# HGRN2 scores in 32-row tiles, state-space decays moved to ScalarE, and state-space outputs in alternating column halves

## The chip, the cores and the metric

The kernel runs on 1 core of one Trainium2 chip. The metric is the device time of one execution in microseconds, lower is better. Engines are named as in the profile: PE is TensorE's matmul side and PEld its weight load, DVE is VectorE, ACT is ScalarE, POOL is GpSimd, SP is SyncE, which issues all DMAs.

## The reference, cut to what matters

A sequence of 512 tokens with 1024 channels goes through two blocks. The first (gated linear attention, a short convolution, sliding-window attention, a gated feed-forward) is not touched by the change. The second puts 16 meta tokens in front, projects, runs two mixers side by side, adds their output projection and runs another feed-forward. The two mixers:

```python
# HGRN2, 8 heads, key and value width 128, f in (0, 1) a forget gate
bcum = cumsum(log f)                       # within a chunk
scores = (q * exp(bcum)) @ (k * exp(-bcum)).T
scores = where(causal, scores, 0)          # s <= r
o_intra = scores @ v
o_inter = (q * exp(bcum)) @ state ; state = exp(blast) * state + k_end.T @ v
...
# Mamba-2 (state space), 16 heads of width 64 in 2 groups, state 128
a_cum = cumsum(dt * a)                     # within a chunk, falling
seg   = a_cum[i] - a_cum[j]
l_mat = exp(where(i >= j, seg, -inf))
y_diag = ((c @ b.T) * l_mat) @ (x * dt)
y_off  = (c @ state) * exp(a_cum) ; state = exp(a_cum[-1]) * state + b.T @ (x * dt * exp(a_cum[-1] - a_cum))
y = (y_diag + y_off + d_skip * x) * silu(z)
```

The kernel takes chunks of 128 tokens for both mixers, and the 16 meta tokens as a chunk of their own.

## The kernel before

**Layout.** Activations lie with channels on the 128 partitions and tokens along the free axis: 512 tokens, or 528 with the meta tokens. All large products run in a split form: each operand is cut into a high and a low part of a reduced 32-bit format (`w_hi`, `w_lo`, `u_hi`, `u_lo`), and three products are summed. The order of all work is one list, `STEPS`, made by `schedule()`: products over one 128-column tile of a weight matrix (a *group*, 8 units of 128 x 128, each unit three products in two halves of 264 columns), with *stages* hung behind chosen groups. Every engine walks the same list and does its own part of each entry, so each engine's queue is in the order of `STEPS`, and semaphores tie the queues together. There is no scheduler behind it.

**Weights.** They stream in slabs of 8 units: SP brings a slab into `w_raw`, ACT rounds it to `w_hi`, POOL forms `w_lo`. ACT does this at the start of a group, two slabs ahead of the slab in use.

**Accumulators.** In the second block the groups alternate between two slots in PSUM banks 0 to 3. The stages use banks 4 to 7.

**HGRN2.** For head n the groups are `hf`, `hq`, `hi`, `hg`, and its stages lie behind the next groups: `prep` behind `hg` of the same head, then, behind `hq`, `hi`, `hg` of the next head and `hf` of the one after, the stages `head_a`, `head_b`, `head_c`, `head_d`. For the last head they lie behind `mb 0`, `mb 1`, `mc 0`, `mc 1`.

- `prep` (ACT, DVE) makes `qd2` (queries times decay) and `KC`: for each block of 128 tokens five matrices of keys, of which the first four are the keys scaled to the four 32-token sub-chunks of queries.
- `head_a` on PE makes the scores in bank 4 (for each block four products, each with a whole 128 x 128 tile of `KC` as the loaded operand and 32 columns of `qd2` as the streamed one), and turns (transposes through the identity) the end keys into bank 5 and the values into bank 6. DVE masks the scores into `h_attn`, key on partitions, query along the free axis. ACT copies the turned keys and values to `h_ktok` and `h_vtok` and reports `tok_ok`.
- `head_b` on PE waits for `tok_ok` and `attn_ok`, then makes the state updates in bank 4; DVE folds them into `h_state`.
- `head_c` on PE makes the output in bank 5 from `h_vtok`, `h_attn`, `h_state` and `qz2`.

All of these products are plain fp32: the trace shows two passes, each a weight load and a matmul, for one product, and one pass for a transpose.

**State space.** For t = 0 to 7, two heads each: group `oh t`, `ssm_a`, group `mz t-1` (not for t = 0), `ssm_gate`, `ssm_b`, group `mx t+1`, `ssm_c`, group `oh t+1`.

- `ssm_a` on PE spreads the cumulated decays of the two heads over all partitions (banks 4 and 5, products with 16 rows) and turns x (bank 6). ACT takes exp of them into `m_er`, and the chunk ends into `m_al` and `m_dec` (`row`). DVE then subtracts the per-partition value and clips at zero, block by block, into `m_at` (L1528, 8 instructions, and L1530 for the meta tokens), and forms `m_dte` and `m_dtm` (`diff`). ACT takes exp of all four (`exp`). DVE, meanwhile, multiplies `m_er` by c, and scales x by dt; behind `exp` it makes the second x tile (`xt`, for which PE's `ssm_b` waits) and multiplies `m_at` by the c-b products (`attn`, for which `ssm_c` waits).
- `ssm_b` on PE makes the state updates, DVE folds them into `m_st` (`state`).
- `ssm_c` on PE makes the outputs of the two heads: head 0 of the pair in PSUM partitions 0 to 63, head 1 in 64 to 127, each with a 64-column loaded operand and 128 streamed columns. Before the change all of head 0 comes first, then all of head 1.

**For comparison in the same program.** The first block has two stages with narrow loaded operands: the GLA scores of `head_a` (two products of 64 output rows, in the lower and the upper half, behind one full one), and `swa_c`, where products of 64 output rows alternate between the halves:

```python
for j in js:
    for g in range(SWA_G):
        lo = slice(SWA_HD * g, SWA_HD * (g + 1))
        last = mm(ps[lo, 3, at:at + BLK], s_vtok[:, b - 1 + j, lo], s_PT[:, 2 * g + i, j, :], ...)
```

`mm(out, lhsT, rhs)` is L541 and `turn` is L545 of the kernel before; in the changed one they are L544 and L548. `f` (ACT's activation) is L822 and L832.

## Time and profile before

| | us |
|---|---|
| median of 3 runs | 1980.67 (1979.62 to 1981.73) |
| the profiled execution, its own time | 1978.91 |
| its span in the profile | 1977.1 |
| PE busy | 1860.9 (94%) |
| DVE busy | 933.3 (47%) |
| ACT busy | 720.7 (36%) |
| POOL busy | 698.2 (35%) |
| mean granted TensorE clock, share of full speed | 0.964 |

The profile is of one execution. Its times are from the start of the span, and its own time is 1.81 us over the span and 1.76 us under the median. In its rows, an engine's line gives the start, the length, the instruction (for PE with rows * columns of the loaded operand and the shape streamed) and in brackets the idle time before it with what ended it. A matmul's length holds its way through the array, so where matmuls follow each other the distance between two starts is what one costs, and that is read from the starts of neighbouring rows. The granted clock is 1.00 at 2.4 GHz and 0.50 at 1.2 GHz.

### The profile page before, as it was taken

To read this page: it belongs to the slowest core of one execution; us is meant where nothing else is said; L and a number is where in the kernel's file an instruction comes from. 1 tells how busy PE (TensorE), PEld (TensorE's weight loads), DVE (VectorE), ACT (ScalarE), POOL (GpSimd) and SP (SyncE) were. 2 spreads that over 40 slices of the span, in tenths; PEclk is the share of its full clock that TensorE was granted. 3 is DMA by queue.
4 is the path that set the end of the run, shared out by engine and by line. 5 is a ranking of instruction groups with operands and counts; after the bars stand their busy time and mean duration, and the time that the engine had idled before them with its cause. 6 is when DMAs were issued, how large, how long until landed. Compare 5 with 4: busy or idle time off the path is not lost.

```text
span 1977.1 us, 26889 instructions
## 1 busy us (share of the span) xinstructions
PE 1860.9 (94%) x11004; PEld 1610.6 (81%) x11004; DVE 933.3 (47%) x1424; ACT 720.7 (36%) x1034; POOL 698.2 (35%) x290
## 2 busy tenths in 40 slices
PE   5999999999999999997899998889998999999997
PEld 3777777778778888886899998778987899999885
DVE  3455523334366656113545455455667265665202
ACT  4444434332343333223346454322332243333221
POOL 2333333344344444442222222212322334444442
PEclk9999999999999999998899998879998999999999
DMA  4222222223223333331221211111211223333331
GB/s 157 75 75 75 75 86 76 85 86 95 87 75 96 96 96 93 99 94 55 65 65 54 73 56 55 54 33 54 65 44 54 75 75 90 93 90 93 96 96 64
DMA packets 44185, 154.15 MB, mean 78 GB/s; under 512 B 5776, under 2 KB 6032, under 8 KB 44064
## 3 DMA queue, kind: packets, MB, share of 16 engines
q1 hardware_dynamic: 44064, 152.44, 25.4%
q8 instruction: 87, 1.43, 0.3%
q14 instruction: 34, 0.28, 0.0%
HBM read 150.33 MB, written 2.10 MB: 77 GB/s over the span
## 4 chain that ended last, share of the span: by engine, by line
PE 83%; DVE 11%; ACT 4%; issue 1%; SPq 0%; ACTq 0%; DMA 0%; DVEq 0%
PE ps L541 81%; DVE arena L1165 4%; ACT arena L822 2%; PE ps L545 2%; DVE full L1311 1%; DVE u_lo L1162 1%; ACT L827 1%; DVE arena L1528 1%; DVE arena L1402 1%; DVE v_hi L1180 0%; DVE arena L1172 0%; DVE h_res L1357 0%; ACTq L1145 0%; DVE arena L1162 0%; ACT r_bc L822 0%
## 5 line engine op out<-in xcount | busy, mean ns | idle before, releaser
L515 POOL TENSOR_TENSOR w_lo<-w_raw,w_hi 128x1024 fp32r<-128x1024 f32 x280 | 690.2, 2468 | 1229.4 <-ACT w_hi L822 1229.3
L541 PE MATMUL ps<-u_hi,w_hi 128*128 128x264 f32 (+3 forms) x2376 | 661.9, 332 | 41.7 <-DVE u_lo L1162 29.9
L541 PE MATMUL ps<-u_hi,w_lo 128*128 128x264 f32 (+3 forms) x2376 | 651.2, 328 | 0.0
L541 PE MATMUL ps<-u_lo,w_hi 128*128 128x264 f32 (+3 forms) x2376 | 648.8, 327 | 0.0
L541 PEld LDWEIGHTS ps<-u_hi,w_hi 128*128 128x128 f32 (+1 forms) x2376 | 403.6, 193 | 98.1 <-issue 44.4
L541 PEld LDWEIGHTS ps<-u_lo,w_hi 128*128 128x128 f32 (+1 forms) x2376 | 403.1, 192 | 37.5 <-issue 0.8
L541 PEld LDWEIGHTS ps<-u_hi,w_lo 128*128 128x128 f32 (+1 forms) x2376 | 404.2, 192 | 35.8 <-issue 1.0
L822 ACT ACTIVATE w_hi<-w_raw 128x1024 fp32r<-128x1024 f32 x280 | 297.0, 1061 | 203.1 <-PE ps L541 167.5
L1172 DVE SCALAR_TENSOR_TENSOR ffn<-ps,par,ffn 128x512 f32<-128x512 f32 (+2 forms) x176 | 132.1, 750 | 192.6 <-ACT ffn L822 187.4
L822 ACT ACTIVATE arena<-ps 128x512 f32<-128x512 f32 (+6 forms) x210 | 91.8, 488 | 323.1 <-PE ps L541 168.0
L541 PE MATMUL ps<-arena 128*64 128x128 f32 (+9 forms) x1212 | 161.0, 289 | 27.9 <-DVE arena L1165 14.6
L541 PEld LDWEIGHTS ps<-arena 128*128 128x128 f32 (+4 forms) x1212 | 139.4, 178 | 51.7 <-issue 18.3
L822 ACT ACTIVATE ffn<-ps,par 128x512 f32<-128x512 f32 x88 | 64.5, 733 | 297.2 <-PE ps L541 297.2
L1165 DVE TENSOR_TENSOR arena<-arena 128x128 f32<-128x128 f32 (+9 forms) x213 | 139.5, 697 | 21.7 <-ACT arena L822 19.8
L1162 DVE TENSOR_TENSOR h_res<-ps,h_res 128x512 f32<-128x512 f32 (+1 forms) x32 | 22.2, 693 | 263.7 <-PE ps L541 263.7
L541 PE MATMUL ps<-a_lo,w_hi 128*128 128x512 f32 x352 | 139.0, 395 | 0.0
L541 PE MATMUL ps<-a_hi,w_lo 128*128 128x512 f32 x352 | 139.0, 395 | 0.0
L541 PE MATMUL ps<-a_hi,w_hi 128*128 128x512 f32 x352 | 139.0, 395 | 0.0
L822 ACT ACTIVATE arena<-arena 128x528 f32<-128x528 f32 (+8 forms) x161 | 77.6, 513 | 154.4 <-DVE arena L1162 81.4
L1180 DVE CAST a_hi<-ffn 128x512 fp32r<-128x512 f32 x44 | 106.3, 2417 | 1.5
L541 PEld LDWEIGHTS ps<-a_hi,w_lo 128*128 128x128 f32 x352 | 66.2, 188 | 15.7
L541 PEld LDWEIGHTS ps<-a_lo,w_hi 128*128 128x128 f32 x352 | 66.2, 188 | 15.7
(129 smaller groups left out, 1528.3 us busy)
## 6 DMA issues: line engine op xcount, KB each, us to landing
w_raw<-weights SPq DMA_DIRECT2D x280, 512.0 KB, 3.6
h_res<-xT SPq DMA_DIRECT2D x4, 512.0 KB, 5.2
outT<-h_res SPq DMA_DIRECT2D x8, 256.0 KB, 2.1
cst<-consts SPq DMA_DIRECT2D x1, 992.0 KB, 9.4
par<-params SPq DMA_DIRECT2D x1, 243.5 KB, 6.8
msk<-cmask SPq DMA_DIRECT2D x1, 64.0 KB, 9.4
h_res<-metaT SPq DMA_DIRECT2D x1, 64.0 KB, 8.6
arena<-w_alpha SPq DMA_DIRECT2D x1, 32.0 KB, 9.1
```

Source lines behind the costliest of these rows:

```text
L515: nc.gpsimd.tensor_tensor(w_lo[:, s % SPL, 0:n], w_raw[:, s % RAW, 0:n], w_hi[:, s % SPL, 0:n], ALU.subtract).then_inc(w_lo_ok, 1)
L541: return nc.tensor.matmul(out, lhsT, rhs, start=start, stop=stop)
L545: return nc.tensor.transpose(out, x, ident[0:k, 0:k])
L822: return nc.scalar.activation(out, in_, func, **k)
L827: nc.scalar.preload_act_table_set("natural_log_exp_and_others")
L1162: return V.tensor_tensor(out, a, b, op)
L1165: return V.tensor_tensor(out, a, b, ALU.mult)
L1172: return V.scalar_tensor_tensor(out=out, in0=a, scalar=s, in1=b, op0=ALU.mult, op1=ALU.add)
L1180: link(V.tensor_copy(hi, x))
L1311: return V.scalar_tensor_tensor(out=out, in0=h_res[:, k, cols], scalar=g, in1=r, op0=ALU.mult, op1=ALU.mult)
L1402: link(V.tensor_tensor_scan(bc2, seg16, lf2, 0.0, ALU.mult, ALU.add))
L1528: V.tensor_scalar(m_at[:, i, b, :], ps[:, 4 + i, b * BLK:(b + 1) * BLK], m_cols[:, 0, b, h0 + i:h0 + i + 1], 0.0, ALU.subtract, ALU.min)
```

## The change

Three edits, all in the second block.

1. **HGRN2 scores.** `head_a` now loads 32 columns of `qd2` and streams the keys: for sub-chunk c the output is rows 32c to 32c+31 of bank 4, and only the 32(c+1) key columns that the mask can keep. The scores come out with the query on the partitions, so DVE masks with `below` (the transposed mask, put beside the old one in `msk`, whose DMA goes from 64 KB to 128 KB). `head_b` on PE turns the four score blocks into bank 5 behind its own products, ACT gets a `head_b` stage that copies them to `h_attnT`, and `head_c` waits for that copy and reads `h_attnT`.
2. **State-space decays.** The ten subtract-and-clip instructions leave DVE. ACT forms them with Relu(-x + bias), reading PSUM: the two of the meta tokens ahead of `row`, the eight of 128 x 128 behind `exp`, then exp with scale -1 over `m_atm` and `m_at`, and reports `decay`, for which DVE waits ahead of its last four products of `ssm_a`. Exp of `m_dte` and `m_dtm` now comes first.
3. **State-space outputs.** `ssm_c` goes block by block and alternates the two heads' halves; the two meta products come at the end.

The first block's code is the same in both kernels, but for the slice of `msk`.

```diff
@@ head_a, PE
-                            q0 = META + at + HG_C * c
-                            mm(ps[:, 4, at + HG_C * c:at + HG_C * (c + 1)], KC[:, b, c * BLK:(c + 1) * BLK],
-                               qd2[:, q0:q0 + HG_C])
+                            q0, n_k = META + at + HG_C * c, HG_C * (c + 1)
+                            mm(ps[HG_C * c:n_k, 4, at:at + n_k], qd2[:, q0:q0 + HG_C], KC[:, b, c * BLK:c * BLK + n_k])
@@ head_b, PE
+                if not gla:
+                    for b in range(NBLK):
+                        last = turn(ps[:, 5, b * BLK:(b + 1) * BLK], h_attn[:, b, :])
+                    last.then_inc(sc_turned, 1)
@@ head_c, PE
+                if not gla:
+                    pe.wait_ge(sc_ok, n - GLA_H + 1)
@@ ssm_c, PE
-                for i in range(2):
-                    rows = slice(M2_P * i, M2_P * (i + 1))
-                    for b in range(NBLK):
-                        out = ps[rows, 4, b * P:(b + 1) * P]
-                        mm(out, m_xt[:, 0, b, rows], m_at[:, i, b, :], stop=False)
-                        mm(out, m_st[:, b, rows], m_er[:, i, META + b * BLK:META + (b + 1) * BLK], start=False)
+                side = [slice(M2_P * i, M2_P * (i + 1)) for i in range(2)]
+                for b in range(NBLK):
+                    out = [ps[rows, 4, b * P:(b + 1) * P] for rows in side]
+                    for i, rows in enumerate(side):
+                        mm(out[i], m_xt[:, 0, b, rows], m_at[:, i, b, :], stop=False)
+                    for i, rows in enumerate(side):
+                        mm(out[i], m_st[:, b, rows], m_er[:, i, META + b * BLK:META + (b + 1) * BLK], start=False)
+                for i, rows in enumerate(side):
                     last = mm(ps[rows, 7, 288:304], m_xtm[0:META, 0, rows], m_atm[0:META, i, :])
@@ head_b, ACT
+                    act.wait_ge(sc_turned, n - GLA_H + 1)
+                    f(h_attnT, ps[:, 5, :].rearrange("p (b t) -> p b t", t=BLK), ACT.Copy).then_inc(sc_ok, 1)
@@ ssm_a, ACT
-                    last = f(m_dec[:, i, :], ends, ACT.Exp)
+                    f(m_dec[:, i, :], ends, ACT.Exp)
+                    last = f(m_atm[0:META, i, :], ps[0:META, 7, 16 * i:16 * i + 16], ACT.Relu, scale=-1.0,
+                             bias=m_colm[0:META, 0, 2 * t + i:2 * t + i + 1])
                 last.then_inc(S["row"], 1)
                 act.wait_ge(S["diff"], t + 1)
-                f(m_at, m_at, ACT.Exp)
-                f(m_atm[0:META], m_atm[0:META], ACT.Exp)
                 f(m_dte, m_dte, ACT.Exp)
                 f(m_dtm[0:META, :], m_dtm[0:META, :], ACT.Exp).then_inc(S["exp"], 1)
+                for i in range(2):
+                    h = 2 * t + i
+                    for b in range(NBLK):
+                        last = f(m_at[:, i, b, :], ps[:, 4 + i, b * BLK:(b + 1) * BLK], ACT.Relu, scale=-1.0,
+                                 bias=m_cols[:, 0, b, h:h + 1])
+                link(last)
+                f(m_atm[0:META], m_atm[0:META], ACT.Exp, scale=-1.0)
+                f(m_at, m_at, ACT.Exp, scale=-1.0).then_inc(S["decay"], 1)
@@ ssm_a, DVE
-                    for b in range(NBLK):
-                        V.tensor_scalar(m_at[:, i, b, :], ps[:, 4 + i, b * BLK:(b + 1) * BLK],
-                                        m_cols[:, 0, b, h0 + i:h0 + i + 1], 0.0, ALU.subtract, ALU.min)
-                    V.tensor_scalar(m_atm[rm, i, :], ...)
...
+                dve.wait_ge(S["decay"], t + 1)
```

PE, `head_a` of the first HGRN2 head, as it stands before (`arena` is the working memory, `cst` the identity, shapes are output rows x columns):

```order
L541 MATMUL ps<-arena 128x32 x4
L545 MATMUL ps<-cst,arena 128x128 x2
L541 MATMUL ps<-arena 128x32 x4
L545 MATMUL ps<-cst,arena 128x128 x2
L541 MATMUL ps<-arena 128x32 x4
L545 MATMUL ps<-cst,arena 128x128 x2
L541 MATMUL ps<-arena 128x32 x4
L545 MATMUL ps<-cst,arena 128x128 x2
L541 MATMUL ps<-arena 16x16
```

The same place in the changed kernel, its first two blocks of four:

```order
L544 MATMUL ps<-arena 32x32
L544 MATMUL ps<-arena 32x64
L544 MATMUL ps<-arena 32x96
L544 MATMUL ps<-arena 32x128
L548 MATMUL ps<-cst,arena 128x128 x2
L544 MATMUL ps<-arena 32x32
L544 MATMUL ps<-arena 32x64
L544 MATMUL ps<-arena 32x96
L544 MATMUL ps<-arena 32x128
L548 MATMUL ps<-cst,arena 128x128 x2
```

The four score products of a block went from four outputs of 128 rows to four of 32 rows, each in its own quarter of the output rows, and the two transposes between the blocks stay. PE, `head_b` of the same head in the changed kernel, with the products of the groups on both sides:

```order
L544 MATMUL ps<-u_lo,w_hi 128x264 x2
L544 MATMUL ps<-arena 128x128 x4
L548 MATMUL ps<-cst,arena 128x128 x4
L544 MATMUL ps<-u_hi,w_hi 128x264 x2
L544 MATMUL ps<-u_hi,w_lo 128x264 x2
```

The row of L548 is new: four transposes between the state updates and the next group. ACT, `ssm_a` of t = 0 before:

```order
L822 ACTIVATE arena<-ps 128x512
L822 ACTIVATE arena<-ps 128x4 x2
L822 ACTIVATE arena<-ps 128x512
L822 ACTIVATE arena<-ps 128x4 x2
L822 ACTIVATE arena<-arena 128x1024
L822 ACTIVATE arena<-arena 16x32
L822 ACTIVATE arena<-arena 128x8
L822 ACTIVATE arena<-arena 16x2
L822 ACTIVATE w_hi<-w_raw 128x1024
```

And in the changed kernel:

```order
L832 ACTIVATE arena<-ps 128x4 x2
L832 ACTIVATE arena<-ps,arena 16x16
L832 ACTIVATE arena<-arena 128x8
L832 ACTIVATE arena<-arena 16x2
L832 ACTIVATE arena<-ps,arena 128x128 x8
L832 ACTIVATE arena<-arena 16x32
L832 ACTIVATE arena<-arena 128x1024
L832 ACTIVATE w_hi<-w_raw 128x1024
```

The small exps of 8 and 2 columns moved ahead of the large one, and eight Relus of 128 x 128 came between; the weight slab's rounding stays behind all of it. PE, `ssm_c` of t = 0 before, ahead of group `oh 1`:

```order
L541 MATMUL ps<-arena 128x128 x4
L541 MATMUL ps<-arena 64x128 x8
L541 MATMUL ps<-arena 64x16
L541 MATMUL ps<-arena 64x128 x8
L541 MATMUL ps<-arena 64x16
```

And in the changed kernel:

```order
L544 MATMUL ps<-arena 128x128 x4
L544 MATMUL ps<-arena 64x128 x16
L544 MATMUL ps<-arena 64x16 x2
L544 MATMUL ps<-v_hi,w_hi 128x258 x2
L544 MATMUL ps<-v_hi,w_lo 128x258 x2
```

The same 16 products now stand in one run, in which the halves alternate, and the two narrow ones stand together behind them.

## Rows read from the trace of the kernel before

**Rows 1.** The page: busy share of each engine, and the chain that ended last.
```profile
PE 1860.9 (94%) x11004; PEld 1610.6 (81%) x11004; DVE 933.3 (47%) x1424; ACT 720.7 (36%) x1034; POOL 698.2 (35%) x290
...
PE 83%; DVE 11%; ACT 4%; issue 1%; SPq 0%; ACTq 0%; DMA 0%; DVEq 0%
```
**Rows 2.** PE's waits from 1290 to 1480 us: us in total, times, longest.
```profile
PE ps L541 <- DVE arena L1172: 7.8, 1, 7.8
PE ps L541 <- DVE arena L1165: 5.1, 5, 1.4
```
**Rows 3.** Timeline of PE, `head_a` of one HGRN2 head.
```profile
1085.15 1.08 PE L541 MATMUL ps<-arena 128*128 128x32 f32 x8 [1.15 <-DVE arena L1165]
1086.07 0.41 PE L545 MATMUL ps<-cst,arena 128*128 128x128 f32 x2
1086.32 0.98 PE L541 MATMUL ps<-arena 128*128 128x32 f32 x8
1087.13 0.41 PE L545 MATMUL ps<-cst,arena 128*128 128x128 f32 x2
...
1089.26 0.42 PE L545 MATMUL ps<-cst,arena 128*128 128x128 f32 x2
1089.61 0.21 PE L541 MATMUL ps<-arena 128*16 128x16 f32 x2
```
**Rows 4.** Timeline of PE, GLA scores: four 64-column passes, then the transposes.
```profile
127.38 0.34 PE L541 MATMUL ps<-arena 128*64 128x64 f32 x4
...
127.65 0.44 PE L545 MATMUL ps<-cst,arena 128*128 128x128 f32 x2
```
**Rows 5.** Timeline of PE: 12 passes inside `ssm_c`, and 14 passes of `swa_c`.
```profile
1336.78 1.47 PE L541 MATMUL ps<-arena 128*64 128x128 f32 x12
...
405.29 0.99 PE L541 MATMUL ps<-arena 128*64 128x128 f32 x14
```
**Rows 6.** Stretches: us, PE busy (instructions), granted clock, DMA share, GB/s.
```profile
1336.51:1340.72 4.21, 4.21 (x38) 1.00 0.28 58
1225.49:1234.32 8.83, 8.80 (x44) 0.50 0.18 61
```
**Rows 7.** Timeline of ACT: the copies ahead of `tok_ok`, then group `hi`.
```profile
1092.79 0.42 ACT L822 ACTIVATE arena<-ps 16x128 f32<-16x128 f32 x2 [1.52 <-DVE arena L1446]
...
1096.03 0.61 ACT L822 ACTIVATE arena<-ps 128x528 f32<-128x528 f32 x1 [1.62 <-PE ps L541]
```
**Rows 8.** Timeline of PE, `ssm_b` and `ssm_c` at t = 2.
```profile
1357.11 1.35 PE L541 MATMUL ps<-arena 16*128 16x128 f32 x8 [1.40 <-DVE arena L1165]
...
1365.74 4.28 PE L541 MATMUL ps<-arena 128*64 128x128 f32 x36
```
**Rows 9.** Timeline of DVE (first three) and ACT (last two) at t = 2.
```profile
1351.35 1.13 DVE L1528 TENSOR_SCALAR arena<-ps,arena 128x128 f32<-128x128 f32 x4 [3.86 <-ACT arena L822]
...
1356.98 3.35 DVE L1165 TENSOR_TENSOR arena<-arena 128x512 f32<-128x512 f32 x4
...
1362.43 1.49 DVE L1172 SCALAR_TENSOR_TENSOR arena<-arena,ps 128x64 f32<-128x64 f32 x6
...
1349.86 1.35 ACT L822 ACTIVATE arena<-ps 128x512 f32<-128x512 f32 x6 [8.18 <-PE ps L545]
1354.02 1.37 ACT L822 ACTIVATE arena<-arena 128x1024 f32<-128x1024 f32 x4 [2.81 <-DVE arena L1162]
```
**Rows 10.** ACT, group with its shape: a 128 x 128 copy out of PSUM.
```profile
L822 ACT ACTIVATE arena<-ps 128x128 f32<-128x128 f32 x1 | 0.3, 277 | 0.1
```
**Rows 11.** Stretches: us, busy of PE, PEld, DVE, ACT, POOL, granted clock, DMA share, GB/s.
```profile
1358.41:1361.82 3.41, 3.41 (x18) 3.41 (x17) 3.14 (x6) 0.00 (x0) 0.61 (x1) 0.50 0.43 151
...
1378.89:1382.30 3.41, 3.41 (x18) 3.41 (x17) 1.68 (x8) 1.35 (x6) 0.00 (x0) 0.50 0.00 0
```
**Rows 12.** The page's DMA issues, KB and us to landing, and ACT at the start.
```profile
msk<-cmask SPq DMA_DIRECT2D x1, 64.0 KB, 9.4
...
15.55 1.06 ACT L822 ACTIVATE w_hi<-w_raw 128x1024 fp32r<-128x1024 f32 x1 [3.60 <-DMA w_raw<-weights]
```

21 lines of the change are left out of this document (12 added, 9 removed).

## The prediction

> **What bounds the kernel now.** I read the page's busy shares and its chain first: TensorE is busy 94% of the span, and 83% of the chain that ended last lies on it [rows 1]. So a change pays where it shortens TensorE's own queue or a wait of TensorE, and nowhere else. Next, PE's waits in the state-space stage [rows 2]: one of 7.8 us, which is `ssm_c` at t = 0 waiting for the state, and five on VectorE's products (L1165), 5.1 us together and 1.4 at most, all ahead of `ssm_b` (the one of t = 2 in [rows 8]). In HGRN2 a wait stands ahead of each `head_a` (1.15 in [rows 3]). Last, the distances between starts inside the stages that are edited.
>
> **Part 1, scores, on TensorE.** From one pair of transposes to the next is 1.06 us (1086.07 to 1087.13 [rows 3]): 0.25 for two transposes, 0.81 for eight passes with 128 loaded columns. After the change a block's eight passes load 32 columns each and write four separate quarters of the output rows. The trace has no 32-row tile; the nearest rows are 64-row tiles in the GLA scores: four passes, 64 columns streamed, two in each half, take 0.27 us from their start to the first transpose (127.38 to 127.65 [rows 4]), as long as two passes of one half, so the halves run beside each other. The widest quarter streams 128 columns in each of two passes. A column costs 0.85 ns: the twelve passes of 128 columns in [rows 5] span 1.47 us, less the 0.27 that one lasts, over 11 steps, is 0.109 us each. So the eight passes of a block cost 0.27 + 2 x 64 x 0.85 ns = 0.38 us if the four quarters run beside each other. A narrow tile behind a full one starts late: two transposes take 0.35 us ahead of one (1089.26 to 1089.61), 0.25 ahead of a full one, so 0.10 more [rows 3]. A block is then 0.38 + 0.25 + 0.10 = 0.73 us against 1.06: 0.33 saved, and over 4 blocks and 8 heads **10.5 us**. Bounds: if the quarters followed each other, the other three would add 2 x (32+64+96) x 0.85 ns = 0.33 us, and nothing is saved; if only neighbours run together, 64 columns twice more is 0.11, and 7 us are saved. I take the full overlap, since both narrow stages of the trace overlap fully, and keep 0 and 10.5 as ends.
>
> **Part 1, what it adds.** Four transposes in `head_b`, at a pass of 0.11 us each: 0.45 per head, **3.6 us** on TensorE, not covered. ScalarE's copy of 512 columns comes behind them, and `head_c` follows a whole group (6 us) later, which hides it. Queued behind it on ScalarE, where it waits for the turned scores some 1.0 us, is the next slab's rounding. That slab is used two groups later, so TensorE does not see it; uncovered it would be 1.6 us per head. A shorter `head_a` brings TensorE to `head_b` earlier, and `head_b` needs `tok_ok`: ScalarE's last copy ends at 1093.21 [rows 7]. TensorE stood at the end of `hi` at about 1095.9; 4 x 0.33 = 1.3 us earlier is 1094.6. No new wait. VectorE's chain to `ready` starts behind `head_c` and `hg`, so the 0.9 to 1.15 us ahead of `head_a` stay.
>
> **The last head** runs `head_a` at the granted clock 0.50: 8.83 us [rows 6], behind a longer wait that stays (it hangs on ScalarE's work for `dt`). At half the clock the same edit saves about twice: **1.1 us** more. Ends 0 and 3, if the clock comes back sooner.
>
> **Part 3, outputs.** `ssm_c` takes 4.21 us [rows 6], 32 passes at 0.109 (3.5) and 0.7 for the four narrow ones and the turns to them. `swa_c` is the same kind of product with the halves alternating: 14 passes span 0.99 us, less 0.27 is 0.72 for seven pairs, 0.11 a pair [rows 5]. So 32 passes are 16 pairs, 1.75 us, and the narrow ones, now together, 0.35: 2.1 us, 2.1 saved, over eight stages **16.9 us**. Ends: 3 (no overlap, only the narrow passes gain) and 17.
>
> Here a page speaks against the change. The trace first: the rows of `swa_c` show pairs of 64-column tiles with 128 rows each at 0.11 us a pair [rows 5]. The Trainium skill's page "TensorE: Matmul & The Clock Gate", Part 3, "The mechanism", says a weight load overlaps running matmuls only when its row group differs, and that matmuls start in strict program order. All these tiles have the same rows, so by that rule nothing in parts 1 and 3 would overlap; what this gives is the first rival. The trace disagrees with it in two stages.
>
> **Part 2, decays.** At t = 2 ScalarE starts at 1349.86, VectorE's subtractions at 1351.35, the last products of `attn` end at 1360.33 [rows 9]: 10.5 us. `xt`, for which `ssm_b` waits, ends at about 1357.0, 7.2 us after the start. VectorE loses ten instructions: 8 in 2.2 us (twice 1.13) and two small ones in 0.2, 2.4 us [rows 9]. ScalarE gains two small Relus ahead of `row`, 0.2 us. So `xt` comes 2.0 to 2.2 us sooner, and every wait ahead of `ssm_b` (1.43 at most) goes: **5.1 us**, lower end 4. The decays: `diff` at about 2.0 us, small exps 0.3, eight Relus at no more than the 0.277 us of a 128 x 128 copy from PSUM [rows 10], 2.2, then 1.1 for the large exp (from the 1.37 of four [rows 9]): `decay` at 5.6 us. VectorE is ready for it at 5.2. So `attn` is at about 9.0 us, 1.5 sooner than before. `ssm_c` at t = 2 starts at 1365.74 [rows 8] and would start 1.4 to 3.1 us earlier; the state, which ended at 1363.92 [rows 9], comes 1.5 earlier, 1362.4. That just suffices; I price it at nothing, with 0.5 us per stage (3.5) as the bad end. At t = 0 the 7.8 us wait is the same VectorE chain and shrinks by 1.5: **1.6 us**, since the next convolution cannot start before ScalarE's part of it, 2.0 sooner.
>
> **The clock.** In the state-space stage the clock falls to 0.50 for 3.4 us seven times between 1320 and 1500. Three of these spells follow directly on a wait of 1.4 us ahead of `ssm_b` (1358.41, 1443.74, 1474.46), four on `ssm_a`, whose products fill 16 rows (as 1378.89) [rows 11]. Each costs half its length, 1.7 us. With the waits the three should go, 5.1 us; that others come or go as the stages shift I cannot exclude. I take **3.4**, ends 0 and 10.
>
> **The start.** `msk` is 64 KB larger [rows 12], in the queue ahead of weight slabs that ScalarE waits for (3.60 us). At the slabs' own landing rate (512 KB in 3.6 us as the page's median) 64 KB is at most 0.45; at the roughly 400 GB/s of that stretch 0.15. I take **0.15** lost.
>
> **Sum.** 10.5 - 3.6 + 1.1 + 16.9 + 5.1 + 1.6 + 3.4 - 0.15 = 34.9 us. The profiled execution of 1978.91 would be 1944.0; it lies 1.76 under the median, so the median should be near 1945.8. I say **1946**.
>
> **Rivals.**
> - *Tiles with the same rows do not overlap* (the rule above). The scores save 0, the outputs 2.9 (narrow passes only), the last head 0: -3.6 + 2.9 + 5.1 + 1.6 + 3.4 - 0.15 = 9.2 saved, 1971. For it: nothing in the rows. Chance 0.04.
> - *Halves overlap, quarters do not.* The quarters would need a pass to overtake up to six others, the halves two; only the latter is in the trace. Scores 0, last head 0: 23.3 saved, 1957. Chance 0.2; with neighbours alone overlapping it is 1950, and that I count with the forecast.
> - *The clock.* The spells of the state-space stage stay or multiply, because `ssm_c` at half its length leaves `ssm_a` a larger share: 3.4 turns into -3.4, 1953. Chance 0.08. Or all spells go: 1939, 0.03.
> - *Each change of tile waits for the one before to drain: slower.* The rows show 0.10 us extra from a full tile to a narrow one [rows 3]. If no overlap came and every change of quarter or half cost x, there are 128 changes in the scores and some 128 in the outputs. The other terms leave 9.2 saved, so from x = 0.036 us it is a loss; at x = 0.10 it is 26 - 9 = 16 us slower, 1997. Against it: `swa_c` changes halves at every product and runs at 0.055 a pass. Chance 0.03.
>
> **Chances and range.** Forecast, 1940 to 1951: 0.62. Quarters not overlapping: 0.20. The clock worse: 0.08, better: 0.03. The page's rule: 0.04; slower: 0.03. The range must reach to the second rival: **1938 to 1958**. A difference of 0.2% (4 us) is about what a measurement of this kernel can tell from no change. Faster 0.96, same 0.01, slower 0.03.
>
> **What would show it.** Right: in `head_a` the transposes of neighbouring blocks 0.73 us apart, `head_b` 0.45 us longer, `ssm_c` near 2.1 us, no wait ahead of `ssm_b`, PE busy lower by 25 to 30 us. The quarters fail if that distance is 1.06 again; the halves fail if `ssm_c` still takes 4 us. A wait of `ssm_c` on the products of `m_at` or on the state at t of 1 or more would say that ScalarE's decays are late. The forecast is wrong above all if the quarters follow each other, or if the low clock shows over more of the state-space stage than before.

## The result and the profile after

The changed kernel takes **1932.03 us** (median of 4, 1930.48 to 1934.71) against 1980.59 for the kernel before in the same comparison (1979.62 to 1981.73): ratio 0.9755, 95% interval 0.9742 to 0.9768. It is 48.6 us faster. The forecast was 34.9 us, 1946, with a range down to 1938, so the sign was right and the size was 14 us too small, outside the range. The profiled execution spans 1931.4 us against 1977.1: 45.7 us, not 48.6, since that of the kernel before is 1.7 us under its median and that of the changed one 1.1 us over.

The page of the changed kernel, engines and chain, answers to [rows 1]:

```profile
PE 1818.5 (94%) x11036; PEld 1557.1 (81%) x11036; DVE 917.6 (48%) x1344; ACT 744.2 (39%) x1122; POOL 698.8 (36%) x290
...
PE 84%; DVE 10%; ACT 3%; issue 1%; SPq 0%; ACTq 0%; DMA 0%; DVEq 0%
```

TensorE is still the bound, and its busy time fell by 42.4 us, not by 25 to 30. PE's waits from 1290 to 1480 us, which answer to [rows 2] (us, times, longest):

```profile
PE ps L544 <- POOL arena L528: 4.0, 1, 4.0
PE ps L544 <- DVE v_lo L1186: 3.4, 2, 2.9
```

All five waits ahead of `ssm_b` are gone (both lines here belong to the end of the stage). `head_a` of a middle head, the timeline of PE (start, us, operation, [idle before]), answers to [rows 3]:

```profile
1077.55 0.43 PE L544 MATMUL ps<-arena 128*32 128x32 f32 x8 [0.86 <-DVE arena L1189]
1077.91 0.44 PE L548 MATMUL ps<-cst,arena 128*128 128x128 f32 x2
1078.27 0.42 PE L544 MATMUL ps<-arena 128*32 128x32 f32 x8
```

A block is 0.72 us long (1077.55 to 1078.27); 0.73 was forecast, 1.06 it was. Now the stretches, each from the start of one stage to the start of the same stage of the next head or pair (us, PE busy, granted clock, DMA share, GB/s). First of the kernel before: first HGRN2 head, second, last head up to `ssm_c` at t = 0, and state-space stages at t = 1 and 2:

```profile
977.37:1016.99 39.62, 38.75 (x267) 0.84 0.13 43
1016.99:1050.93 33.94, 33.08 (x266) 1.00 0.21 63
1225.49:1306.19 80.70, 64.04 (x424) 0.80 0.15 46
1336.51:1365.74 29.23, 27.83 (x202) 0.94 0.18 55
1365.74:1393.56 27.82, 27.82 (x202) 0.94 0.20 58
```

The same of the changed kernel, and last its `ssm_c`, which answers to the first of [rows 6]:

```profile
977.68:1011.91 34.23, 33.36 (x271) 0.95 0.16 49
1011.91:1044.73 32.82, 31.96 (x271) 1.00 0.22 65
1213.44:1288.83 75.39, 58.93 (x428) 0.84 0.16 50
1314.71:1338.87 24.16, 24.16 (x202) 1.00 0.22 66
1338.87:1364.54 25.67, 25.67 (x202) 0.93 0.21 64
...
1338.87:1340.99 2.12, 2.12 (x38) 1.00 0.04 8
```

How to read them: the clock is 1.00 or 0.50, so a stretch of length L with mean c had 2 x (1 - c) x L us of low clock: the first head 12.7 us before and 3.4 after. Over the whole span the clock's own records in the trace add up to 141 us before and 106 after (mean clocks 0.964 and 0.972). Most of what the forecast missed lies in that difference. Where did the 45.7 us between the two spans go?

| stretch | before | after | gained |
|---|---|---|---|
| up to the first HGRN2 head | 977.37 | 977.68 | -0.3 |
| first head | 39.62 | 34.23 | 5.4 |
| six further heads | 208.5 | 201.5 | 7.0 |
| last head, to `ssm_c` at t = 0 | 80.7 | 75.4 | 5.3 |
| from there to `ssm_c` at t = 7 | 202.9 | 175.1 | 27.7 |
| from there to the end | 468.1 | 467.5 | 0.6 |

### The profile page after: what moved, and what is told of

Its sections match the earlier page's. It is cut to its first block, busy times and chain, and to the rows that moved or that the text cites. A ratio compares the mean times of both kernels' runs of the same rounds, so it can differ in the third digit from the quotient of the medians.

```text
span 1931.4 us, 26981 instructions
## 1 busy us (share of the span) xinstructions
PE 1818.5 (94%) x11036; PEld 1557.1 (81%) x11036; DVE 917.6 (48%) x1344; ACT 744.2 (39%) x1122; POOL 698.8 (36%) x290
## 4 chain that ended last, share of the span: by engine, by line
PE 84%; DVE 10%; ACT 3%; issue 1%; SPq 0%; ACTq 0%; DMA 0%; DVEq 0%
PE ps L544 82%; DVE arena L1189 3%; ACT arena L832 2%; PE ps L548 2%; DVE full L1335 1%; DVE u_lo L1186 1%; ACT L837 1%; DVE arena L1426 1%; DVE v_hi L1204 0%; DVE arena L1196 0%; DVE h_res L1381 0%; ACTq L1169 0%; ACT r_bc L832 0%; DMA w_raw<-weights 0%; DVE v_lo L1186 0%
## 5 line engine op out<-in xcount | busy, mean ns | idle before, releaser
L544 PE MATMUL ps<-u_hi,w_hi 128*128 128x264 f32 (+3 forms) x2376 | 656.5, 330 | 42.4 <-DVE u_lo L1186 30.5
L544 PEld LDWEIGHTS ps<-u_hi,w_hi 128*128 128x128 f32 (+1 forms) x2376 | 399.4, 191 | 99.1 <-issue 45.0
L544 PEld LDWEIGHTS ps<-u_lo,w_hi 128*128 128x128 f32 (+1 forms) x2376 | 398.8, 190 | 37.2 <-issue 0.6
L544 PEld LDWEIGHTS ps<-u_hi,w_lo 128*128 128x128 f32 (+1 forms) x2376 | 399.1, 190 | 35.9 <-issue 1.0
L832 ACT ACTIVATE arena<-ps 128x512 f32<-128x512 f32 (+7 forms) x218 | 97.1, 485 | 288.7 <-PE ps L544 146.3
L544 PE MATMUL ps<-arena 128*64 128x128 f32 (+13 forms) x1212 | 120.8, 283 | 22.3 <-DVE arena L1189 9.3
L544 PEld LDWEIGHTS ps<-arena 128*64 128x64 f32 (+6 forms) x1212 | 91.5, 155 | 49.0 <-issue 21.7
L544 PEld LDWEIGHTS ps<-a_hi,w_hi 128*128 128x128 f32 x352 | 66.2, 188 | 15.8
```

Of the source, the lines that this page charges most:

```text
L544: return nc.tensor.matmul(out, lhsT, rhs, start=start, stop=stop)
L832: return nc.scalar.activation(out, in_, func, **k)
```

## Experiments

Theory: the direct terms of the sum hold, and the missing 14 us are TensorE's clock, low for less time since TensorE pauses less and works less in the stages edited. Rivals: a direct term (one of passes and waits alone) was too small; the parts help each other in another way; the smaller low clock is the luck of where pauses fall in time.

### The parts alone

`e1_scores` is the kernel before with part 1 alone, `e2_decays` with part 2, `e3_outputs` with part 3, `e4_decays_outputs` with parts 2 and 3; the edits are those of the diff above.

> The kernel before with the first edit alone (scores in 32-row tiles, turned). Theory, direct work and clock: a head_a is 1.57 us shorter and a head_b 0.44 longer, 1.13 net, 9.0 us over eight heads; and the two head_a that run at the granted clock 0.50 (the first and the last) let the clock come back sooner, 4.2 and 3.0 us as in the changed kernel. Together 16 us: 1964 to 1966, with the first low spell behind 976 us only some 3.4 us long against 13.65. Rival, the clock's return has nothing to do with the tiles (it hangs on where the stages lie): 9 us, 1971 to 1973, and the first low spell stays near 13 us.

Measured: 1961.91 us (1961.42 to 1966.11), ratio 0.9912 (0.9895 to 0.9929), 19.5 us faster where 16 were expected. The first two heads and the last (start to start as above):

```profile
977.45:1012.40 34.95, 34.09 (x271) 0.92 0.15 47
1012.40:1045.22 32.82, 31.96 (x271) 1.00 0.21 65
1214.00:1290.80 76.80, 59.28 (x428) 0.83 0.17 49
```

At full clock a head is 1.12 us shorter (33.94 to 32.82; 0.86 forecast), the first one 4.7 us shorter, since its low clock fell from 12.7 to 5.6 us. Part 1 alone does this. The two low-clock figures are 2 x (1 - clock) x length.

> The kernel before with the second edit alone (decays on ScalarE). Theory: the five waits ahead of ssm_b go (5.1 us), the wait of ssm_c at t = 0 shrinks by 1.3 us, and the three low-clock spells that follow waits of 1.4 us go (5.1 us): 11.5 us, 1968 to 1971. Rival, spells come elsewhere as the stages move: 6.4 us, 1973 to 1975, with as many spells as before. Second rival, the decays arrive late and ssm_c waits: less than 4 us, above 1976.

Measured: 1969.11 us (1967.91 to 1970.24), ratio 0.9941 (0.9926 to 0.9956), 12.3 us faster. Two of its state-space stages:

```profile
1473.69:1499.95 26.26, 26.26 (x201) 1.00 0.21 61
...
1336.48:1364.29 27.81, 27.81 (x202) 0.94 0.19 58
```

No wait stands ahead of `ssm_b`. A stage is 26.26 us at full clock, and 1.55 more with a spell of low clock in it; the trace has four such spells without a wait in front.

> The kernel before with the third edit alone (outputs in alternating halves). Theory: ssm_c takes 2.12 us against 4.21, 16.7 us over eight stages; the waits ahead of ssm_b stay at 5.1 us in all and with them the spells behind them: 1962 to 1966. Rival: VectorE's chain, which ended 0.3 to 2 us ahead of ssm_c, becomes what the next stages wait for, since they come 2.1 us sooner: waits ahead of ssm_a or ssm_b grow and less than 12 us are saved, 1969 or more.

Measured: 1968.97 us (1967.08 to 1969.26), ratio 0.9939 (0.9924 to 0.9953), 12.5 us faster: less than expected, and about what the rival said, by which the waits grow. `ssm_b` of one stage, a whole stage, and PE's waits from 1290 to 1480 us:

```profile
1327.27 1.55 PE L541 MATMUL ps<-arena 16*128 16x128 f32 x8 [1.43 <-DVE arena L1167]
...
1390.28:1417.45 27.17, 25.77 (x202) 0.94 0.18 58
...
PE ps L541 <- DVE arena L1167: 8.5, 6, 1.4
```

The shorter `ssm_c` brings TensorE to `ssm_b` before VectorE has `xt`: the wait of 1.4 us is now in every stage from t = 1 on, seven in all (six of them in that window), and behind each stands a spell of 3.4 us (clock 0.94 over 27.17 us). Five of the seven stages last 27.15 to 27.2 us.

> The kernel before with the second and third edits. Theory, the edits add: the changed kernel less what the scores give, 48.6 - 16 = 32 us saved, 1947 to 1950. If the clock's share in the state-space stage (8.9 us in the changed kernel) hangs on where that stage lies, this kernel, in which it lies 12 to 16 us later than in the changed one, shows another number of low spells than the two there: 1953 to 1956 without that share.

Measured: 1947.55 us (1943.86 to 1949.01), ratio 0.983 (0.9815 to 0.9845), 33.9 us faster, where the two alone add up to 24.8. Two stages:

```profile
1356.74:1380.91 24.17, 24.17 (x202) 1.00 0.23 67
1380.91:1405.09 24.18, 24.18 (x203) 1.00 0.23 66
```

This closes the account of a stage. 26.26 - 24.17 = 2.09 us is `ssm_c` (2.1 forecast). The outputs alone give 27.17 = 24.17 + 1.42 for the wait + 1.58 for the low clock. So part 3 needs part 2: alone it exposes VectorE's chain, and part 2 shortens just that. Part 1 alone and parts 2 and 3 together add up to 53.4 us, 4.8 more than the whole change. The median of the kernel before is 0.8 us higher in this comparison, which counts twice; the rest isn't settled.

### Is it the luck of a place?

In `e6_after_later` and `e7_before_later` the changed kernel and the one before repeat the first product of one group seven times:

```diff
+                        for a, b in cuts * 7 if n == 0 and j == 0 and (kind, idx) == ("hf", 3) else ():
+                            mm(out[:, a:b], wt, x[:, a:b])
                         for a, b in cuts:
                             last = mm(out[:, a:b], wt, x[:, a:b], start=(n == 0 and j == 0),
```

> The changed kernel with seven extra repeats of the first product's two column halves in the group ('hf', 3), ahead of the products themselves (14 matmuls of 264 columns, about 0.12 us each, so 1.7 us more, on TensorE's path), which moves everything behind it by 1.7 us; their result is overwritten. Theory (low clock follows TensorE's pauses, wherever they fall): the low spells stay what they were in the trace of after, 108.5 us in all give or take two spells of 3.4 us, and the time is 1932.0 + 1.7 = 1933.7 us (1931 to 1937). Rival (how much low clock a kernel gets hangs on where its pauses fall in time, so that the smaller low clock of after, 108.5 us against 142.9 us of before, is the luck of a place): the low spells come to 120 us or more or under 100 us, and the time lies outside 1930 to 1938 us.

> The kernel before with the same seven extra repeats in the group ('hf', 3), 1.7 us more for all that comes behind. Theory (low clock follows the pauses): low spells 142.9 us in all give or take two spells of 3.4 us, five waits of 1.4 us ahead of ssm_b remain, time 1980.6 + 1.7 = 1982.3 us (1980 to 1985). Rival (luck of a place): low spells come down towards the 108.5 us of after with nothing else changed, and the time falls by up to 17 us, to 1965 to 1975 us.

Measured: 1936.78 us (1936.5 to 1937.87), ratio 0.9791 (0.9777 to 0.9806), and 1982.99 us (1981.16 to 1984.2), ratio 1.0019 (1.0009 to 1.003). Less than 1 us of the 1.7 showed in the head concerned (33.61 for 32.82 us, 34.61 for 33.94), since the wait ahead of `head_a` took up the rest. Low clock in all is 117 us for the changed kernel and 148 us for the one before (the clock's records again): 11 and 7 us more than unmoved, and still 31 apart. The 11 us are more than the two spells that the theory allowed. In `e7_before_later` a spell of 6.8 us stands in a head that had none in the kernel before, behind a pause of the same length (1.14 us for 1.15), and makes it 3.0 us longer than the 33.94 of its neighbours:

```profile
1085.71:1122.66 36.95, 36.08 (x266) 0.91 0.17 58
```

So place moves some 10 us of low clock, 2 to 5 us of time, from one variant to another; it doesn't explain the 34 us between the two kernels. The other kernels say the same of the state-space stages, which begin in them at other times. Spells that start between `ssm_c` at t = 0 and at t = 7: 7 in the kernel before and in `e7_before_later`, 6 in `e1_scores`, 7 in `e3_outputs`, 4 in `e2_decays`; with parts 2 and 3 together 2, 1, 1, 2 and 0 (changed kernel, `e4_decays_outputs`, `e5_one_quarter`, `e6_after_later`, `e8_scores_first`). The first head lies ahead of the repeats, so these two kernels do not move it.

### The wait put back

`e9_wait_back`: the changed kernel, VectorE's first product of `xt` done four times.

```diff
+                for _ in range(3):
+                    link(mul(m_xt[:, 0].rearrange(split, i=2), xt, bc(m_cols[:, 1, :, h0:h0 + 2], M2_P)))
                 mul(m_xt[:, 0].rearrange(split, i=2), xt, bc(m_cols[:, 1, :, h0:h0 + 2], M2_P))
```

> The changed kernel, with VectorE computing the first scaled input (128x512, 0.65 us with its hand-over) four times in place of once in every ssm_a, so that xt comes 2.0 to 2.2 us later; the slack ahead of ssm_b is 0.5 us in the trace of after (xt at 1331.05, ssm_b could start at 1331.6), so a wait of about 1.5 us comes back ahead of seven ssm_b. Nothing else is changed, and the value computed is the same. Theory (each such wait brings a low spell of 3.4 us behind it, worth 1.7 us, as seven did in the run with the outputs alone): 7 x 1.5 = 10.5 us of waits, and four to five spells more than the three that after has there, 7 to 8.5 us: 1932 + 18 = 1950 us (1947 to 1954). Rival (the wait costs its own length and no more): 1932 + 10.5 = 1942.5 us (1941 to 1945). A second rival (ssm_c waits for the state as well, which also comes 2 us later): over 1955 us.

Measured: 1952.26 us (1950.28 to 1954.16), ratio 0.9865 (0.9848 to 0.9883). VectorE's delayed products, `ssm_b` behind them, and two stages:

```profile
1335.19 3.04 DVE L1189 TENSOR_TENSOR arena<-ps,arena 128x512 f32<-128x512 f32 x5
...
1339.34 0.90 PE L544 MATMUL ps<-arena 16*128 16x128 f32 x4 [1.46 <-DVE arena L1189]
...
1348.00:1375.20 27.20, 25.72 (x202) 0.94 0.21 60
1375.20:1402.39 27.19, 25.73 (x202) 0.94 0.20 59
```

Seven waits of 1.46 to 1.84 us, 10.7 us in all, stand against a kernel that is 20 us slower. From `ssm_c` at t = 0 to t = 7 it is 17.4 us (192.5 for 175.1); 1.4 of the rest lie in the first head, ahead of the edit. Six of the waits have a spell of 3.4 us behind them, and such a stage grows from 24.16 to 27.20 us, by 1.46 and 1.58. No work was added on TensorE, so a pause of that kind costs twice its own length here.

### Do the quarters run beside each other?

`e5_one_quarter` writes all four products of a block to rows 0 to 31, so that its scores and outputs are other values; the number and the shapes of its products are the same:

```diff
-                            mm(ps[HG_C * c:n_k, 4, at:at + n_k], qd2[:, q0:q0 + HG_C], KC[:, b, c * BLK:c * BLK + n_k])
+                            mm(ps[0:HG_C, 4, at:at + n_k], qd2[:, q0:q0 + HG_C], KC[:, b, c * BLK:c * BLK + n_k])
```

> The changed kernel with the four score products of a block all written to rows 0 to 31 of the scores, in place of rows 0 to 31, 32 to 63, 64 to 95 and 96 to 127: the scores of HGRN2 and with them its outputs are other values, while the number of instructions, their shapes and their data are the same; only the column tile of the array that each product uses is changed. Theory (the four products of a block overlap since they use four different column tiles): they follow one another, the distance from block to block grows from 0.72 to 1.0 to 1.1 us, and 32 blocks cost 9 to 12 us: 1941 to 1945 us. Rival (the products follow one another anyway, and the 0.72 us come from their being short): the distance stays 0.72 us and the time 1931 to 1934 us.

Measured: 1943.59 us (1943.32 to 1944.33), ratio 0.9824 (0.9811 to 0.9838). Two blocks:

```profile
1084.37 0.74 PE L544 MATMUL ps<-arena 128*32 128x32 f32 x8 [0.86 <-DVE arena L1189]
...
1085.41 0.75 PE L544 MATMUL ps<-arena 128*32 128x32 f32 x8
```

From block to block 1.04 us in place of 0.72, a head 34.10 in place of 32.82: the same products in one quarter of the array's columns follow one another. The overlap of quarters is what part 1 lives on.

### The clock taken back

If low clock costs half its length, filling TensorE's pauses should give it back. `fill(n, bank)` is n matmuls of ones by ones (128 columns) into a PSUM bank free at that place. `e11_filled`, `e12_filled_less` and `e14_filled_ahead` are the changed kernel with it behind the sums of `norm1`, in `head_a`, `ssm_bc`, `ssm_c` (between its waits for `attn` and for the state) and, in the last form alone, `ssm_sum`. That form:

```diff
+                fill({"norm1": 24}.get(which, 0), 4)
...
             def head_a(n):
-                pe.wait_ge(ready, n + 1)
                 gla = n < GLA_H
-                evacuated(pe, GROUP_OF[("gv", n) if gla else ("hi", n - GLA_H)])
                 if n:
                     pe.wait_ge(state_ok, n)
+                    fill({GLA_H: 12, GLA_H + HG_H - 1: 20}.get(n, 0), 4)
                     pe.wait_ge(o_ok, n)
                     pe.wait_ge(r_ok, n)
+                pe.wait_ge(ready, n + 1)
+                evacuated(pe, GROUP_OF[("gv", n) if gla else ("hi", n - GLA_H)])
...
+                fill(0 if g else 28, 4)
...
+                fill(0 if t else 22, 4)
...
+                fill(14 * g, 5)
```

> The changed kernel, with matmuls that do nothing useful (128 columns of ones by ones, two passes, about 0.11 us each, into a PSUM bank that is free there) in TensorE's five long waits: 24 behind the sums of norm1 (wait 7.5 us), 24 ahead of the first HGRN2 head (3.7 us), 40 ahead of the last one (5.5 us), 56 ahead of ssm_bc(0) (7.8 us) and 44 ahead of ssm_c(0) (7.4 us). They fill 2.6 to 6.2 us of each wait, and what they would cost if they reached past the wait is 0. Theory (the clock falls because TensorE pauses, and the low clock behind the pause is what costs): of the spells of after at 978.4 (3.4 us), 1210.5 (10.2), 1251.5 (10.2), 1272.0 (3.4) and 1285.6 (6.8), 34.1 us in all, most go: 20 to 34 us of low clock less, 10 to 17 us of time, 1915 to 1922 us. Rival (the low clock there is not tied to the pause, or is given for the kind of work): the spells stay, and the time is 1931 to 1934 us. Second rival (the fillings run at 1.2 GHz and reach past the waits): up to 5 us slower, 1937 us.

Measured: 1946.38 us (1945.31 to 1948.19), ratio 0.984 (0.9825 to 0.9855), 14 us slower than the changed kernel. A matmul of this type is two passes of 0.11 us, not one; 56 of them:

```profile
1259.58 12.77 PE L544 MATMUL ps<-ones 128*128 128x128 f32 x112
```

> The same as the run before with matmuls that do nothing useful in TensorE's five long waits, with their size put right: the trace of that run shows 0.111 us for each of the two passes, 0.223 us for a matmul, twice what the counts were made for, so that 56 of them took 12.8 us in a wait of 7.8 us, and the 40 ahead of the last head stood behind the wait and not in it. Now 24 behind the sums of norm1 (5.4 us in a wait of 7.5), 12 ahead of the first HGRN2 head (2.7 in 3.7), 20 ahead of the last (4.5 in 5.5, ahead of its waits for ready and for hi), 28 ahead of ssm_bc(0) (6.2 in 7.8), 22 ahead of ssm_c(0) behind its wait for attn (4.9 in 6.3). Theory (the low clock follows the pause): the spells of after at 978.4, 1210.5, 1251.5, 1272.0 and 1285.6, 34.1 us in all, go but for at most two of 3.4 us, no filling reaches past its wait, and the time falls by 12 to 17 us: 1915 to 1921 us. Rival (the fillings only move the low clock to a later place, so that it falls on work instead of the wait): low clock falls by under 15 us in all, and the time is 1925 to 1932 us. Second rival (some filling is late after all): above 1932 us.

Measured: 1932.2 us (1931.59 to 1934.65), ratio 0.9768 (0.9755 to 0.9782). The filling ahead of the last head stands behind the wait that it should fill, and runs at low clock:

```profile
1213.90 6.70 PE L544 MATMUL ps<-ones 128*128 128x128 f32 x40 [5.58 <-ACT arena L840]
```

The last head started at 1220.53, not 1213.44, and 7.1 us lost there covered what was won elsewhere.

> The changed kernel with matmuls that do nothing useful in six waits of TensorE, as in the run before the last, but the 20 ahead of the last HGRN2 head stand ahead of its wait for the last head's norm (o_ok, r_ok), which the trace of that run shows to be the one that lasts 5.5 us, and 14 more (3.1 us) stand ahead of ssm_sum(1)'s wait for POOL (3.9 us). Theory (low clock taken away gives half its length back): the last head starts 5 to 7 us earlier than in that run, gains of 1.2 us at the first head and 4.2 us between last head and ssm_c(0) stay, and two spells fewer behind ssm_sum(1) give 2 to 3 us: 1932.2 - 7 - 2 = 1923 us (1920 to 1926). Rival (the low clock taken away gives nothing back in time): 1930 to 1933 us. Second rival (the 5.5 us were needed: TensorE's work in that wait slows ScalarE, which it waits for): above 1933 us.

Measured: 1930.1 us (1927.21 to 1932.86), ratio 0.9746 (0.9733 to 0.976): no measurable gain on 0.9755, although the mean clock is 0.98, 30 us less low clock. First head, second head, last head:

```profile
979.34:1012.37 33.03, 31.95 (x271) 1.00 0.16 50
1012.37:1045.38 33.01, 31.94 (x271) 1.00 0.21 65
1214.85:1289.83 74.98, 68.56 (x527) 0.93 0.17 50
```

The first head is 1.2 us shorter than in the changed kernel (34.23), as 3.4 us of low clock are worth. But over the last head 14 us of low clock less gave 0.4 us. The row that says why is `head_b` of that head:

```profile
1226.33 1.99 PE L544 MATMUL ps<-arena 16*128 16x128 f32 x7 [2.18 <-ACT arena L841]
```

TensorE, now at full clock, arrives earlier and waits 2.2 us for ScalarE's copies, a wait that the changed kernel hasn't. Up to `ssm_c` at t = 0 this stretch hangs on VectorE's and ScalarE's chain; low clock there lies beside it. And the second head is 33.01 us long for 32.82: in this kernel `head_a`'s waits stand in another order, and its idle time is 1.07 us for 0.86. Also, the first head starts 1.7 us later (979.34 for 977.68), which nothing here explains.

### Versions that go further

`e8_scores_first` is the changed kernel with the loops of `head_a` parted:

```diff
...
+                    for b in range(NBLK):
+                        at = b * BLK
+                        for c in range(SUB):
+                            q0, n_k = META + at + HG_C * c, HG_C * (c + 1)
+                            mm(ps[HG_C * c:n_k, 4, at:at + n_k], qd2[:, q0:q0 + HG_C], KC[:, b, c * BLK:c * BLK + n_k])
+                    for b in range(NBLK):
+                        at = b * BLK
+                        turn(ps[:, 5, at:at + BLK], KC[:, b, SUB * BLK:(SUB + 1) * BLK])
+                        last = turn(ps[:, 6, at:at + BLK], vf2[:, META + at:META + at + BLK])
```

> The changed kernel with the HGRN2 blocks in another order in head_a: all 16 score products (128 rows by 32 columns) of the four blocks first, then the eight transposes (128 by 128), in place of four times (four products, two transposes). Theory (the changes between the 32-column and the 128-column shape are part of the 0.72 us from block to block): six of eight changes of shape go in each head, at 0.09 to 0.10 us each, 0.5 to 0.7 us a head in eight heads, 4 to 6 us: 1926 to 1928 us. Rival (the time is all in the products and transposes themselves): no change, 1931 to 1933 us. Second rival (mask and copies of VectorE and ScalarE start at the end of head_a either way, but the two transposes of a block used to hide behind the products): up to 3 us slower, 1935 us.

Measured: 1928.85 us (1925.85 to 1932.24), ratio 0.9749 (0.9736 to 0.9763). The interval meets that of the changed kernel. In the trace all 16 products take 1.01 us (1077.88 to 1078.89) and the eight transposes the same:

```profile
1077.88 1.08 PE L544 MATMUL ps<-arena 128*32 128x32 f32 x32 [0.86 <-DVE arena L1192]
1078.89 1.09 PE L548 MATMUL ps<-cst,arena 128*128 128x128 f32 x8
...
1077.92 2.59 DVE L1223 TENSOR_SCALAR arena<-arena 128x528 f32<-128x528 f32 x1
1080.57 0.30 PEld L544 LDWEIGHTS ps<-u_hi,w_hi 128*128 128x128 f32 x2 [0.41 <-DVE arena L1223]
...
1077.88:1110.25 32.37, 31.38 (x270) 1.00 0.21 66
```

That is 2.03 us to the small products where it was 2.90, but the head is only 0.45 us shorter: 0.4 come back as a pause ahead of the next group, `hi`. The rows of VectorE and of TensorE's weight load say why. `hi` needs the accumulator of `hf`, which VectorE gives back with one instruction of 2.59 us (L1223); it ends at 1080.51, and the group starts 0.06 us later. In the changed kernel the same instruction ends at 1113.01 and the group starts at 1113.56, so there were some 0.5 us to win here and no more. `e15_first_ahead` agrees: 1075.61 and 1075.66.

`e13_first_filled`, `e15_first_ahead` are this kernel with the fillings of `e12_filled_less` and `e14_filled_ahead`.

> Both together: score products first, and the five waits filled. Theory: the two act in different places, so the sum of the two gains, 16 to 23 us: 1909 to 1916 us. Rival (a shorter head_a makes the clock fall again in the heads, or the gain of head_a lies in the wait ahead of the last head only): 1916 to 1921 us.

Measured: 1928.67 us (1927.89 to 1929.17), ratio 0.9747 (0.9734 to 0.9761), the misplaced filling in it.

> The kernel with the score products first, and the same six waits filled. Theory: 1928.85 us of the run with the score products first, less the same 8 to 10 us as in the run of this batch against the changed kernel: 1919 us (1916 to 1923). Rival (nothing back): 1927 to 1930 us.

Measured: 1924.75 us (1923.49 to 1927.87), ratio 0.9724 (0.9711 to 0.9737), 4 us better than `e8_scores_first`, where 8 to 10 were expected and the low clock is 37 us less (66 us for 102). `e16_rows_too` adds, in `ssm_a`, a second row group for the second head of a pair, for which dt and its running sums are computed a second time in partitions 32 to 47:

```diff
+                    r0 = 32 * i
-                    pick = ident[0:M2_H, 2 * t + i:2 * t + i + 1].broadcast_to((M2_H, P))
-                    mm(ps[:, 4 + i, :], pick, ac_t[0:M2_H, META:T2])
+                    pick = ident[r0:r0 + M2_H, r0 + 2 * t + i:r0 + 2 * t + i + 1].broadcast_to((M2_H, P))
+                    mm(ps[:, 4 + i, :], pick, ac_t[r0:r0 + M2_H, META:T2])
...
```

> The same, and in ssm_a the row products of the two heads of a pair (16 rows, 512 columns, two passes of 0.52 to 0.53 us, 1.19 us from one head to the next with its small product in the trace of after at 1322.79 and 1323.98) use two different row groups of the array: partitions 0 to 15 for the one and 32 to 47 for the other, where dt and its running sums are computed a second time. Theory (they run side by side): 1.0 to 1.1 us less in each of eight ssm_a, 8 to 9 us: 1910 us (1907 to 1915). Rival (two row groups of 16 rows do not overlap, or the ones that read it wait for it no less): 1917 to 1921 us. Second rival (the 48 rows of dt make ScalarE's work longer, or its sums late): above 1921 us.

Measured: 1913.57 us (1911.31 to 1916.33), ratio 0.9664 (0.965 to 0.9677), the fastest of all: 11 us better than `e15_first_ahead`, 18 better than the changed kernel. `ssm_a`'s row products, and a stage at full clock:

```profile
1313.47 1.32 PE L545 MATMUL ps<-arena,cst 16*128 16x512 f32 x8
...
1328.52:1351.64 23.12, 23.09 (x201) 1.00 0.23 70
```

They took 2.45 us in the changed kernel. A stage is 23.12 us for 24.26 (1330.05 to 1354.31 in `e15_first_ahead`): 1.14 gained in a stage. From `ssm_c` at t = 0 to t = 7 that is 10.4 us with a low clock of 6.8 us less (163.4 for 173.8), and the stretch of the last head, which holds the first `ssm_a`, is 1.8 shorter.

## Why the prediction was wrong

**Scores, 10.5 - 3.6 us.** Right, a little small. The block is 0.72 us (0.73). `head_a` is 3.18 us long with its small products and was 4.75, so 1.57 us saved where 1.32 was forecast; with 0.44 for the transposes of `head_b` (0.45) a head at full clock gives 1.12, not 0.86: 2 us more over eight heads. The first rival, the rule of the Trainium skill's page "TensorE: Matmul & The Clock Gate", Part 3, "The mechanism", fell: all these tiles load 128 rows, and both quarters (0.72 against 1.04 us in one quarter) and halves (`ssm_c` 2.12 us for 4.21) run beside each other. The second, that quarters do not overlap though halves do, fell with `e5_one_quarter`.

**The last head, 1.1 us more.** Too small: 5.3 us in all, of which 1.12 are the head's own saving and 1.26 the chain at t = 0 (80.66 to 79.40 in the run with the decays alone; 1.6 forecast). 2.9 are left where 1.1 stood. `head_a` ran at half the clock, as forecast, but there it went from 8.83 us to 5.24 (1213.44 to the next group at 1218.68), 3.6 saved where a head at full clock saves 1.57, so 2.0 more and not 1.1. The other 0.9 stand beside 8.7 us of low clock that went; what made them isn't settled.

**Outputs, 16.9 us.** Right: 2.09 us a stage, 16.7. Some 1.5 us of it are not to be seen at the end: behind the last `ssm_c` TensorE now waits longer for VectorE's split of `v` (5.3 us for 4.0), so the stretch to the end is 0.6 us shorter and not 2.1. In `e4_decays_outputs` that wait is 4.1 us and the stretch 466.6, so this loss isn't in every kernel.

**Waits ahead of `ssm_b`, 5.1 us.** Right. They went in the run with the decays alone, and came back in all stages in the one with the outputs alone. `ssm_c` never waited for the decays on ScalarE at t of 1 or more; for the state it waited once in `e2_decays` and once in `e6_after_later`, 0.3 us each. At t = 0 the wait gave 1.26 us where 1.6 were forecast.

**The start, 0.15 us lost.** Not settled: the first HGRN2 head starts 0.3 us later than before, but among the runs without part 1 that start alone lies anywhere from 975.8 to 978.1.

**The clock, 3.4 us: this step failed.** The step said that three spells of the state-space stage go with their waits, that the others stay, and that no other place gains; what the first head's low clock would give back it put at nothing, without a reason. Measured:
- First head: 39.62 to 34.23 is 5.4 us, 1.1 of it direct, so 4.3 for 9 us of low clock less. I had looked only at the state-space stage for the clock, and had not asked what a shorter `head_a` does to the low clock behind the wait ahead of it. Part 1 alone brings it. Some of the size is the luck of this execution: `e6_after_later` and `e9_wait_back` have the same code up to there and show 35.6 us with 6.8 of low clock.
- State-space stages: 202.9 to 175.1 is 27.7 us; seven times 2.09 is 14.6, the waits are 5.1, so 8.0 are left for 28.3 us of low clock turned into 10.4. The three spells behind a wait go, but so do spells on `ssm_a`, of which two are left. In the run with the decays alone, where `ssm_c` is still 4.2 us long, four stay; with both parts one. That the single file of half-width products brought them is what the runs suggest, not what they show.
- 4.3 + 8.0 = 12.3 for 3.4 forecast, 8.9 more. With 1.8 in the last head and 2.1 in the scores, and less 2.2 in the outputs, the wait at t = 0 and the start, that is 10.6 us, and the two profiled executions are 10.8 further apart than forecast. The other 2.9 of the 14 us are between those executions and the medians, of which no profile tells.
- The range's end of 10 for the clock was too near, and by the prediction's own price too: seven spells at 1.7 us are 11.9.

**How much low clock costs.** Forecast: half its length. Measured where TensorE is what is late: 5.68 us for 12.4 to 12.7 in the first head before (39.62 less the 33.94 at full clock), 1.41 for 3.4 after, 3.0 for 6.8 in `e7_before_later`, 1.5 to 1.6 for 3.4 in the stages: 0.41 to 0.46. In the last head, where TensorE waits for others three times, 14 us less gave 0.4. So the total (141 to 106 us) may not be halved and taken as time: it gives 17 us, and the stretches where it counts give 12 to 14. My expectations for the filled kernels made just this mistake again.

**Chances.** "All spells go: 1939" had 0.03 and "the clock worse: 1953" had 0.08. The rows gave no reason to lean to the worse side, and the range should have reached at least as far below the forecast as above.

## What to carry to other kernels

A part that shortens TensorE's queue at a place with a low granted clock behind a pause saves more than its own passes, so read the clock of every stretch that is edited, on both sides of the wait. Price low clock at 0.4 to 0.46 of its length only where no wait for another engine comes soon behind it, and at next to nothing where one does. When one edit shortens an engine's work and another the chain that it will then wait for, make both: apart parts 2 and 3 gave 24.8 us, together 33.9. Before a stage is shortened further, read when the next group could start at the earliest: in `e8_scores_first` half of what was saved met an accumulator that VectorE hadn't yet given back.

## What the runs showed of the hardware

- Pauses of 1.4 us on TensorE ahead of a 1.35 us stage of 16-row products were followed by 3.41 us at clock 0.50 in seven of seven stages of `e3_outputs`, six of seven of `e9_wait_back`, three of three in the kernel before and two of three in `e1_scores`. Pauses of 0.86 us ahead of `head_a` were followed by none in six heads of the changed kernel, but in `e2_decays` and `e3_outputs` the one at the second head had 6.83 us of it some 3 us behind (1018.18 and 1017.66), and that head took 37.0 us for 33.95. The length of a pause alone doesn't decide.
- Four tiles of 32 columns with the same 128 rows overlap: eight passes, whose widest streams 128 columns, in 0.36 us against 0.68 in one quarter (1077.55 to 1077.91, 1084.37 to 1085.05).
- Two products of 16 rows and 512 columns in two row groups take the time of one: `ssm_a`'s row products, the small ones with them, went from 2.45 to 1.32 us (two of 1.19 before, by the starts).
- In the filled kernels, where the waits of `ssm_c` and `head_a` are written in another order, a state-space stage is 24.25 us for 24.16 and a head 33.01 for 32.82; I have not found why. With the scores first no such loss shows in a head (32.35 in `e15_first_ahead`, 32.34 in `e8_scores_first`), since the next group waits for VectorE either way.
